# Hybrid encoder on one core: projection columns regrouped, projection products split in halves over the scan steps, two attention heads started earlier

## The reference, cut to what matters

```python
for i in range(DEPTH):                       # 2
    h = rmsnorm(x, g_mix[i])
    u, q, k, v = jnp.split(h @ w_in[i], splits, axis=-1)        # 4 x 512 columns
    y_ssm = ssm_mixer(u, ...)                # scan forward and backward, gelu, glu, rmsnorm
    y_att = diff_attention(q, k, v, ...)     # 4 heads, two softmax maps each
    x = x + jnp.concatenate([y_ssm, y_att], axis=-1) @ w_out[i]
    h = rmsnorm(x, g_ffn[i])
    x = x + (swiglu(h, ...) if i % 2 == 0 else moe_swiglu(h, ...))
...
s1 = jnp.einsum('bqhd,bkhd->bhqk', q_blk[..., 0, :], k1) + bias      # and s2 with k2
attn = jax.nn.softmax(s1, axis=-1) - lam * jax.nn.softmax(s2, axis=-1)
o = rmsnorm(jnp.einsum('bhqk,bkhe->bqhe', attn, vh), g_subln) * (1.0 - lambda_init)
```

## Time and profile before

| | us |
|---|---|
| three runs: median (lowest, highest) | 1628.25 (1622.36, 1638.08) |
| the profiled execution, own time | 1645.27 |
| its span, first to last instruction | 1643.4 |
| mean granted TensorE clock, share of full | 0.957 |
| mixer of layer 0, loc to the start of atn1 | 45.5 to 189.3 |
| mixer of layer 1, loc to the start of atn1 | 455.8 to 591.8 |

### The profile page before, as it was taken

The page is one execution under the profiler, slowest core; times in us unless marked ns, Lnnn a source line. Parts: engine busy times, 40 slices in busy tenths (PEclk is TensorE's granted clock), DMA queues, the critical chain, the costliest instruction groups (busy, mean ns, idle before and its releaser), DMA issues.

```text
span 1643.4 us, 21157 instructions
## 1 busy us (share of the span) xinstructions
PE 1558.2 (95%) x7000; PEld 1247.1 (76%) x7000; DVE 1250.6 (76%) x1299; ACT 1012.3 (62%) x1180; POOL 156.5 (10%) x116
## 2 busy tenths in 40 slices
PE   6999889999899987999999999999999999999896
PEld 6866558888786746787888887887887887887685
DVE  6667554543766855888888888888898888888795
ACT  3458343432446734677777777777777777777673
POOL 0345100000045600000000000000000000001000
PEclk9787899999979798999999999999999999999998
DMA  8322234552712123899999999999999999999991
GB/s 329 130 91 84 79 137 176 184 199 77 285 61 103 36 106 127 312 375 360 381 374 366 380 372 367 382 371 367 372 376 367 383 366 366 388 379 351 367 365 69
DMA packets 68237, 442.05 MB, mean 269 GB/s; under 512 B 8416, under 2 KB 14944, under 8 KB 18528
## 3 DMA queue, kind: packets, MB, share of 16 engines
q1 hardware_dynamic: 64880, 429.60, 68.8%
q0 software_dynamic: 2304, 8.19, 1.4%
q10 hardware_dynamic: 1008, 3.67, 0.6%
HBM read 432.52 MB, written 5.77 MB: 267 GB/s over the span
## 4 chain that ended last, share of the span: by engine, by line
PE 85%; DVE 7%; DMA 3%; ACT 2%; issue 2%; POOL 0%; SPq 0%; DVEq 0%; ACTq 0%; POOLq 0%
PE ps L1597 43%; PE ps L1579 21%; PE ps L1399 3%; PE ps L1504 2%; PE ps L1456 2%; PE ps L1543 2%; PE ps L1426 2%; PE ps L1528 2%; DVE wsplit L1042 2%; PE ps L1557 2%; PE ps L1437 2%; DMA cw<-cmat 1%; PE ps L1474 1%; ACT wsplit L574 1%; PE ps L1482 1%
## 5 line engine op out<-in xcount | busy, mean ns | idle before, releaser
L1042 DVE TENSOR_TENSOR wsplit<-raw,wsplit 128x2048 fp32r<-128x2048 f32 x369 | 835.7, 2289 | 130.2 <-ACT wsplit L574 120.6
L1597 PE MATMUL ps<-wsplit,xh 128*128 128x512 f32 x2144 | 709.4, 396 | 7.0 <-DVE hv L1068 3.4
L574 ACT ACTIVATE wsplit<-raw 128x2048 fp32r<-128x2048 f32 x369 | 694.3, 1915 | 2.4 <-issue 2.2
L1597 PEld LDWEIGHTS ps<-wsplit,xh 128*128 128x128 f32 x2144 | 403.3, 188 | 89.0 <-DVE wsplit L1042 3.7
L1597 PE MATMUL ps<-wsplit,xl 128*128 128x512 f32 x1072 | 418.5, 390 | 0.0
L1579 PE MATMUL ps<-wsplit,hidh 128*128 128x512 f32 x1072 | 310.6, 393 | 20.1 <-DVE hidl L1049 20.1
L1579 PEld LDWEIGHTS ps<-wsplit,hidh 128*128 128x128 f32 x1072 | 201.7, 189 | 65.8 <-DVE wsplit L1042 20.0
L1597 PEld LDWEIGHTS ps<-wsplit,xl 128*128 128x128 f32 x1072 | 202.3, 189 | 38.6
L582 ACT ACTIVATE hidh<-ps 128x256 fp32r<-128x256 f32 (+1 forms) x123 | 49.7, 404 | 266.1 <-PE ps L1557 266.0
L1579 PE MATMUL ps<-wsplit,hidl 128*128 128x512 f32 x536 | 166.9, 393 | 0.0
L1579 PEld LDWEIGHTS ps<-wsplit,hidl 128*128 128x128 f32 x536 | 101.6, 189 | 21.5
(11 more groups left out here) (254 smaller groups left out, 1256.2 us busy)
## 6 DMA issues: line engine op xcount, KB each, us to landing
raw<-wffn SPq DMA_DIRECT2D x369, 1024.0 KB, 6.9
mixw<-wmix SPq DMA_DIRECT2D x12, 2048.0 KB, 7.9
cyt<-bmat SPq DMA_DIRECT2D x2, 2048.0 KB, 13.8
cw<-cmat SPq DMA_DIRECT2D x2, 2048.0 KB, 23.1
results<-ybuf ACTq DMA_DIRECT2D x7, 512.0 KB, 7.1
qk<-wglu SPq DMA_DIRECT2D x2, 1024.0 KB, 5.2
X<-x_in SPq DMA_DIRECT2D x2, 512.0 KB, 4.5
loc<-dmat SPq DMA_DIRECT2D x2, 512.0 KB, 23.9
```

The source lines that it names most:

```text
L574: nc.scalar.activation(wh[slot], raw[:, PLACE[slot]], ACT.Copy).then_inc(s["hi_done"], 1)
L1042: tt(wl[slot], raw[:, PLACE[slot]], wh[slot].bitcast(F32), ALU.subtract).then_inc(s["lo_done"], 1)
L1597: ins = mm(ps[:, b], x2[:, fx, t * P:(t + 1) * P], w2[slot][:, f * 512:(f + 1) * 512], start=(fx == 0 and i == 0), stop=(fx == KT - 1 and ...
```

## The change

- The columns of w_in are regrouped on the host: chunk 1 holds q and k of heads 0 and 1, chunk 2 all of v, chunk 3 q and k of heads 2 and 3. `zqkv0`, `zqkv1` are now q and k of heads 0 and 1; `zqkv2`, `zqkv3` are v; `zqkv4`, `zqkv5` are q and k of heads 2 and 3.
- `ZQKV_AT` has a first and a last step for each unit. A unit whose two differ is computed in halves (`/0` and `/1`), one per step; `zqkv1` is split within step 0, around `loc1`.
- `HEAD_AT` goes from 6, 8, 10, 12 to 3, 5, 9, 11. With it oms0 moves from step 14 to 11, atn0 from 16 and 17 to 13 and 14, oms1 from 18 to 17, atn1 from 19 and 20 to 18 and 19; there are 21 steps.
- AT and diag move from hT to bw[:, 0] and bw[:, 1] (B matrices whose steps are over), osq to two slices of cyt, one buffer for both pairs of heads.
- Within a step the map, turn and head units now stand ahead of the projection, and oms ahead of these.

```diff
-ZQKV_AT = (0, 1, 3, 4, 6, 8)
+ZQKV_AT = ((0, 0), (0, 0), (1, 2), (3, 4), (5, 6), (7, 7))
-HEAD_AT = [6, 8, 10, 12]
+HEAD_AT = [3, 5, 9, 11]
...
 def beside(i):
+    if i == 0:
+        return [("zqkv0", "A"), ("loc0", "D"), ("zqkv1/0", ""), ("loc1", "D"), ("zqkv1/1", "A")]
     work = []
-    for k, at in enumerate(ZQKV_AT):
-        if at == i:
-            work.append((f"zqkv{k}", "A"))
-            if k == 0:
-                work += [(f"loc{d}", "D") for d in range(2)]
+    for b in range(HEADS // 2):
+        if i == OMS_AT[b]:
+            work.append((f"oms{b}", "A"))
...
+    for k, (first, last) in enumerate(ZQKV_AT):
+        if i == first == last:
+            work.append((f"zqkv{k}", "A"))
+        elif i == first:
+            work.append((f"zqkv{k}/0", ""))
+        elif i == last:
+            work.append((f"zqkv{k}/1", "A"))
...
-        AT = hT[:, 0:2]
-        diag = hT[:, 2:4].rearrange("p m (q t) -> p m q t", q=TT)
-        osq = hT[:, 4:8].rearrange("p (k a) t -> p k a t", k=2)
+        diag = bw[:, 0].rearrange("p r d m -> p (r d m)").rearrange("p (m q t) -> p m q t", m=2, q=TT)
+        AT = bw[:, 1].rearrange("p r d m -> p (r d m)").rearrange("p (k t) -> p k t", k=TT)
+        osq = cyt[:, 0:2]
...
+                for j in parts:
                     for f in range(KT):
+                        if k // 2 != 1:
+                            n = 2 * (k % 2) + j
+                            ins = mm(ps[:, bank(u), j * 256:j * 256 + 256], mixw[:, c % 2, f, n * P:(n + 1) * P], hT[:, f, :],
+                                     start=(f == 0), stop=(f == KT - 1))
+                        elif f // (KT // 2) == j:
+                            t = k - 2
+                            ins = mm(ps[:, bank(u), :], hT[:, f, t * P:(t + 1) * P], mixw[:, c % 2, f, :],
+                                     start=(f == 0), stop=(f == KT - 1))
...
+    cols = np.arange(4 * SW).reshape(8, SW // 2)[[0, 1, 2, 4, 6, 7, 3, 5]].reshape(-1)
+    wmix = np.concatenate([chunks(a["w_in"][:, :, cols], KT, 4), chunks(a["w_out"], KT, 2)], 1)
```

More of the change, by code:

```diff
@@ L83, in beside @@
             work.append((f"head{h}", "A"))
+    for k, (first, last) in enumerate(ZQKV_AT):
[5 more added lines that the diff above has]
+            work.append((f"zqkv{k}/1", "A"))
     for b in range(HEADS // 2):
-        if i == OMS_AT[b]:
-            work.append((f"oms{b}", "A"))
         if 0 <= i - ATN_AT[b] < 2:
@@ L94 @@
 UNITS = ([("norm", "D"), ("norm", "A")] * 2 + [("zu", "A")] * 2 + [("bt", "A")] * PAIRS
-         + [w for i in range(STEPS) for w in beside(i)] + [("glu", "A")] * 2 + [("out", "D")] * 4 + [("fnorm", "D"), ("fnorm", "A")] * 2)
+         + [(n.split("/")[0], who) for i in range(STEPS) for n, who in beside(i) if who] + [("glu", "A")] * 2 + [("out", "D")] * 4 + [("fnorm", "D"), ("fnorm", "A")] * 2)
 UL = len(UNITS)
@@ L565, in attention @@
                     nc.scalar.activation(cat[:, FT + h], ps[:, bank(u), 0:SEQ], ACT.Copy, scale=col[:, 15:16])
-                    nc.scalar.activation(osq[:, h // 2, h % 2], ps[:, bank(u), 0:SEQ],
+                    nc.scalar.activation(osq[:, h % 2], ps[:, bank(u), 0:SEQ],
                                          ACT.Square).then_inc(s["emptied_act"], 1)
@@ L648, in _ @@
                     for k in range(6):
-                        if ZQKV_AT[k] != i - 1:
+                        if ZQKV_AT[k][1] != i - 1:
                             continue
@@ L653, in _ @@
                         pb = ps[:, bank(u)]
-                        if k < 4:
-                            h = 2 * (k % 2)
-                            if k < 2:
+                        if k // 2 != 1:
+                            h = k // 4 * 2
+                            if k % 2 == 0:
                                 for a in range(2):
@@ L663, in _ @@
                         else:
-                            nc.scalar.activation(v[:, k - 4], pb, ACT.Copy).then_inc(s["emptied_act"], 1)
+                            nc.scalar.activation(v[:, k - 2], pb, ACT.Copy).then_inc(s["emptied_act"], 1)
                     if i - 1 in OMS_AT:
@@ L1024, in head_norm @@
                 heads = cat[:, FT + 2 * b:FT + 2 * b + 2]
-                link(nc.vector.reciprocal(osq[:, b], osq[:, b]))
-                tt(heads, heads, osq[:, b], ALU.mult).then_inc(s["normed"], 1)
+                link(nc.vector.reciprocal(osq, osq))
+                tt(heads, heads, osq, ALU.mult).then_inc(s["normed"], 1)
             def attention_out(l, b, at):
@@ L1467, in attention @@
                     if h == 0:
-                        empty_wait(unit(l, "zqkv3"))
+                        empty_wait(unit(l, "zqkv1"))
                         pe.wait_ge(s["in_exact"], 32)
+                    elif h == 2:
+                        empty_wait(unit(l, "zqkv5"))
                     r = slice(HD * m, HD * m + HD)
@@ L1484, in attention @@
                 elif stage[:4] == "head":
-                    empty_wait(unit(l, "zqkv5"))
+                    empty_wait(unit(l, "zqkv3"))
                     empty_wait(unit(l, f"turn{h}"))
@@ L1493, in attention @@
                     empty_wait(unit(l, f"head{2 * h + 1}"))
-                    ins = mm(ps[:, bank(u)], ones, osq[:, h], start=True, stop=True)
+                    ins = mm(ps[:, bank(u)], ones, osq, start=True, stop=True)
                 else:
@@ L1531, in output, with zqkv @@
                     ins.then_inc(s["unit_done"], 1)
-            def zqkv(l, k):
-                u = unit(l, f"zqkv{k}")
-                if k % 2 == 0:
-                    mix_wait(pe, chunk(l, 1 + k // 2))
-                if k < 4:
-                    project(l, u, chunk(l, 1 + k // 2), k % 2)
-                else:
+            def zqkv(l, name):
+                k, parts = int(name[4]), (0, 1) if "/" not in name else (int(name[-1]),)
+                u, c = unit(l, f"zqkv{k}"), chunk(l, 1 + k // 2)
+                if 0 in parts:
+                    if k % 2 == 0:
+                        mix_wait(pe, c)
                     free(u)
-                    t = k - 4
+                for j in parts:
                     for f in range(KT):
-                        ins = mm(ps[:, bank(u), :], hT[:, f, t * P:(t + 1) * P], mixw[:, chunk(l, 3) % 2, f, :],
-                                 start=(f == 0), stop=(f == KT - 1))
+                        if k // 2 != 1:
+                            n = 2 * (k % 2) + j
[5 more added lines that the diff above has]
+                                     start=(f == 0), stop=(f == KT - 1))
+                if 1 in parts:
                     ins.then_inc(s["unit_done"], 1)
@@ L1617, in _ @@
                         if stage[:4] == "zqkv":
-                            zqkv(l, int(stage[4:]))
+                            zqkv(l, stage)
                             if stage == "zqkv0":
@@ L1810, in chunks @@
         return w.reshape(DEPTH, kt, P, n, 512).transpose(0, 3, 2, 1, 4)
-    wmix = np.concatenate([chunks(a["w_in"], KT, 4), chunks(a["w_out"], KT, 2)], 1)
+    cols = np.arange(4 * SW).reshape(8, SW // 2)[[0, 1, 2, 4, 6, 7, 3, 5]].reshape(-1)
+    wmix = np.concatenate([chunks(a["w_in"][:, :, cols], KT, 4), chunks(a["w_out"], KT, 2)], 1)
     wglu = chunks(a["w_glu"], FT, 1)[:, 0]
```

2 lines of the change are left out of this document (1 added, 1 removed).

## The result

The changed kernel takes 1643.24 us (median of 17 runs, 1635.10 to 1651.00). The kernel before, run as often beside it, takes 1632.28 us (1619.86 to 1652.58). The ratio is 1.0064, 95% interval [1.0035, 1.0092]. The forecast was 1619 us with a range of 1603 to 1637: the time lies outside, and the sign is wrong. By the bound of 1% it is still no difference.

A forecast was written before the change was run, and what follows sets the result against it. TensorE, busy 95% of the span and losing most to low clock, was taken to bound the kernel. Gains of 19.7 us less 8 for the clock gave 12, less 3 for the median: 1628 - 9 = 1619 us, range 1603 to 1637.

The forecast's parts named there:

- The shift to the median: Whole kernel: profiled execution 17.0 us above the median; half the runs lack its fall, so 3 us of gain fall away.
- The sum: Both mixers: 13.7 us gained in layer 0 and 6.0 in layer 1, 19.7 together, less 8 for the clock.
- Part 1: Steps 0 and 1: projection halves around loc's second half keep it at the high rate; gain 4.9 us per layer.
- part 2: Steps 1 to 7: same products in another order, TensorE sets the pace, 52.2 us; step 8 begins at 116.4 us.
- Part 3: Steps 8 to 15: VectorE bounds, 45.1 us; last scan ends at 162.2 and atn1 starts at 175.6 in layer 0.
- waits for ScalarE 3.6: Steps 8 to 15: VectorE's estimated waits, from four table loads more per layer ahead of the sines; 3.6 us.
- The wait before atn1: End of the mixer: TensorE's wait for head_norm grows from 5.0 to about 7.5 us.
- What the clock takes back: Both mixers: 1.5 us per layer around turn 2 and 2.5 in steps 9 to 11; 8 us in all.
- Turn 2: Its wait for diagonal 2 grows from 2.3 to about 3.7 us; a clock fall there costs 1.5 us per layer.
- The fall behind a map: Mixer: a matter of chance in one execution; layer 0 paid 6.3 us that layer 1 did not.
- The steady clock: Rival: only waits pull the clock down, so maps 2 and 3 stay high; 1605 to 1611 us, chance 0.22.
- The slower rival: Steps 8 to 13: TensorE bounds again at the low clock, 20 us per layer; about 1648 us, chance 0.10.

The follow-up runs named there:

- loc_alone: Kernel before with only the second input-projection unit issued in two halves around the second local product; ratio to before 1.0008.
- b_again: The unchanged kernel before, profiled once more for a second trace; 1627.8 us at clock 0.971.
- no_recip0: Changed kernel without the reciprocal in head_norm of heads 0 and 1, 3.35 us of VectorE per layer; ratio to before 1.0066.
- b_oms13: Kernel before with oms0 issued right behind the product whose squares it needs, at the end of step 13, so TensorE waits; ratio to before 1.0013.
- head2_10: Changed kernel with the third head started at step 10 instead of 9, the fourth still at 11; ratio to before 1.0052.
- oms0_later: Changed kernel with oms0 at step 12 instead of 11, and atn0 one step later with it; ratio to before 1.0075.
- filler: Changed kernel with four dummy products per layer ahead of oms0's wait; ratio to before 1.0040.
- head2_1012: Changed kernel with heads at steps 3, 5, 10 and 12, the last two as before; ratio to before 1.0059.
- b_more: Kernel before with the second projection unit split around the second local product, and dummies ahead of turns 1 and 2 and the last attention output; ratio 0.9957.

## Why the prediction was wrong, by its steps

- **The shift to the median** is the step that failed first: "I take it that half of the runs lack it, so 3 us of gain fall away". The whole sum, -12, was made against one execution at clock 0.957. The median of the changed kernel is 2.0 us under that execution and 11.0 over the median of before: 13.0 us lie between these two gains, where 3 were allowed. Of the 24 us between 1619 and 1643.24 this is 10; 4 more are the median of before (1632.28, not 1628.25); the last 10 are the sum itself, 12 forecast and 2 measured.
- **The sum.** By TensorE's timeline the two mixers, loc to atn1, are 4.9 us shorter than in the earlier trace rows, where 19.7 - 8 = 11.7 were forecast. 3.1 us of what is missing are in layer 0 up to step 8 (mostly the fall behind the second map), 3.8 from step 8 to atn1 (64.4 twice, for 62.5 twice); the rest of the 10 lies outside the mixers and between this profile and the median.
- **Part 1** named the mechanism rightly (second half of loc 3.68 us, high) and mis-sized it: 9.8 us over both layers forecast, 1.9 us less time on average in loc_alone, within its uncertainty. One layer of b_again has no fall in loc to save, nor has layer 1 of the changed kernel. The 18.6 us of layer 0 came out (45.62 to 64.24) by two errors that cancel, 5.96 for 4.9 in the first half of loc and 4.46 for 5.4 in the half product: the 6 rows of one microsecond are too many for the low rate, since 12.41 us for 64 products, 17 of them in the first 2, leave about 4.5 per us. In part 2 the terms listed add up to 51.9 rather than 52.2, which decides nothing.
- **Part 3** failed in "VectorE more, so VectorE bounds": no_recip0. The last scan ended at 169.4 instead of 162.2, and the end was set by TensorE, which had no wait from oms0 (139.32) to the last out (176.3, said 167), at a clock of 0.53 from 138 to 160 us; no run kept that clock up and left all else as it was. Of "waits for ScalarE 3.6" I counted only VectorE's; the one that mattered was TensorE's at oms0, 3.50 us, behind head 2's exponentials. The wait before atn1 was right: 7.35 us, 7.5 said.
- **What the clock takes back** was 8 us against the profiled execution; the clock term against a typical run is 10. Turn 2 was named as the place; its wait did not appear, oms0's did. The fall behind a map came in both layers (6.48 and 6.49 us), where I had counted it as chance.
- **The rivals.** The steady clock is out. The slower rival named the right resource, TensorE at the low level in steps 8 to 13 (0.53 from 138 to 160 us, and TensorE on the chain that ended last), and a right reason to doubt the forecast; with +1% it was too far, and 0.10 was too little.

The rest of -1.2 us says that next to nothing of the forecast gain is left beside the clock; it doesn't say how much of the 19.7 us was gain over falls of that one execution. The Trainium skill, TensorE: Matmul & The Clock Gate (section "Why this matters for your kernels"), puts such drops down to idle gaps. Here that agrees in part: all six kernels with dummies in waits have a higher clock than the kernel that each was made from. It disagrees in b_oms13, in layer 0 of head2_10 (low for 23 us without a wait over 0.2), and in part in loc. There the level fell in a busy microsecond, but not unrelated to a wait: over the two layers of all 19 profiles, loc fell in all 15 layers where TensorE had waited 0.85 to 1.22 us for cw right ahead of it, in none of 15 where it had waited 0.64 us or less, and in 5 of 8 between. The prediction's "everything ahead of it is unchanged" overlooked that this wait varies from run to run (1.12 and 0.45 us in the two layers of b_again, with 12.69 and 7.36 us of loc behind it). Whether an earlier cw would save these 5 us was not tried.

**Open.** Which property of the heads' steps lowers the clock. Filling either the last wait or oms0's restores it to that of the before runs beside, but dummies raise the clock of the unchanged kernel too, so that is no proof that the waits lowered it; and oms0_later, head2_10 and b_oms13 speak against the wait at oms0. The longer last wait (7.35 against 4.98 us) goes with the low clock in every kernel without dummies that has the last head at step 11, but filler has it too at +0.0012, and head2_1012 has 6.75 us at -0.0016; no run changed that wait alone without dummies. The order of units within a step was not tried alone either. Whether the dummies act by filling the wait or as full-height products was not told apart either.

## What to carry to other kernels

Before a gain is read off one profiled execution, set its time and its clock beside the other runs: where time follows the clock from run to run, a fall seen once is not a loss to be won back. Split a result into clock and rest, since a reordering with equal work can lose 10 us in the clock alone. When attention steps are pulled forward, follow each eviction from PSUM in ScalarE's order too; and ask what will cover the last norm, since work done early is no longer there.

## What the runs showed of the hardware

- Runs of one kernel spread over 2% (1618 to 1653 us) with the mean clock from 0.979 to 0.954, 13.5 us per hundredth.
- The same 64 local products took 7.36 us in one layer and 12.69 in the other layer of one execution (b_again), with TensorE busy throughout; it had waited 0.45 us right ahead of them in the first case and 1.12 in the second.
- The level can fall and stay low for 23 us without a wait of over 0.2 us: head2_10, layer 0, from 135 us, behind a map of 64-row products.
- TensorE with dummy products in its waits (b_more: 22 more per execution) runs at a mean clock of 0.9778, the kernel before beside it at 0.9659, and it is the faster of the two (ratio 0.9957, with the split of loc_alone in it as well).
